# Split weights woven in pairs of chunks, and 64 bytes of padding behind the token-major tile

## The reference, cut to what matters

```
q, k, v, ga, uf, gf, zc, bc, cc, gc = split_cols(hx @ w_in, PROJ_SIZES)   # 1024 x 2816
a, b = jnp.split(h @ w_in, 2, axis=-1)                                    # 1024 x 5632
return (jax.nn.silu(a) * b) @ w_out                                       # 2816 x 1024
yx, yc = even_mixer(...)    # in: 1024 x 3088, out: 1024 x 1024
yx, yc = odd_mixer(...)     # in: 1024 x 3104, out: 1024 x 1024
```

## Time and profile before

| | |
|---|---|
| median of three runs | 2315.22 us |
| the profiled execution's own time, first to last instruction (its span) | 2314.2 us |
| TensorE matmuls busy | 2227.1 us, 19320 instructions |
| weight loads busy | 2091.2 us, 19320 instructions |
| VectorE busy | 1145.4 us |
| ScalarE busy | 846.8 us |
| GpSimd busy | 176.3 us |
| mean granted TensorE clock | 0.987 |
| share of the DMA queue that loads the weights | 46.1% of 16 engines' span |

### The profile page before, as it was taken

The page is one execution under the profiler, slowest core; times in us unless marked ns, Lnnn a source line. Parts: engine busy times, 40 slices in busy tenths (PEclk is TensorE's granted clock), DMA queues, the critical chain, the costliest instruction groups (busy, mean ns, idle before and its releaser), DMA issues. The chain is left out here.

```text
span 2314.2 us, 46991 instructions
## 1 busy us (share of the span) xinstructions
PE 2227.1 (96%) x19320; PEld 2091.2 (90%) x19320; DVE 1145.4 (49%) x1930; ACT 846.8 (37%) x1384; POOL 176.3 (8%) x150
## 2 busy tenths in 40 slices
PE   6999999899999999998999999999999999999998
PEld 5986798799999999976999999999999998979998
DVE  5227375653433445456653333454343446487665
ACT  4226454632221233248432222243232234455444
POOL 0003112100000010501200000010000010001000
PEclk9999999999999999999999999999999999999999
DMA  9853544445676244520354666242233233225573
GB/s 297 234 167 86 172 133 104 128 147 154 186 216 186 86 131 117 149 80 28 102 175 141 190 207 189 84 126 85 81 114 94 86 96 101 74 82 146 168 202 112
DMA packets 515900, 315.76 MB, mean 136 GB/s; under 512 B 16035, under 2 KB 513274, under 8 KB 515622
## 3 DMA queue, kind: packets, MB, share of 16 engines
q1 hardware_dynamic: 515160, 313.45, 46.1%
q10 hardware_dynamic: 590, 0.16, 0.0%
HBM read 312.50 MB, written 1.06 MB: 135 GB/s over the span
## 5 line engine op out<-in xcount | busy, mean ns | idle before, releaser
L1118 PE MATMUL ps<-h_hi,w_hi 128*128 128x256 f32 x3376 | 728.0, 280 | 3.5 <-DVE h_lo L1726 1.7
L1118 PE MATMUL ps<-h_lo,w_hi 128*128 128x256 f32 x3376 | 720.6, 278 | 0.0
L1118 PE MATMUL ps<-h_hi,w_lo 128*128 128x256 f32 x3376 | 720.6, 278 | 0.0
L1118 PEld LDWEIGHTS ps<-h_hi,w_hi 128*128 128x128 f32 x3376 | 537.8, 189 | 22.9 <-issue 21.6
L1118 PEld LDWEIGHTS ps<-h_lo,w_hi 128*128 128x128 f32 x3376 | 539.4, 189 | 0.1
L1118 PEld LDWEIGHTS ps<-h_hi,w_lo 128*128 128x128 f32 x3376 | 537.9, 189 | 0.0
L1960 DVE TENSOR_TENSOR w_lo<-stage,w_hi 128x1024 fp32r<-128x1024 f32 x227 | 285.0, 1258 | 441.5 <-ACT w_hi L1467 440.9
L1467 ACT ACTIVATE w_hi<-stage 128x1024 fp32r<-128x1024 f32 x227 | 236.6, 1055 | 334.4 <-PE ps L1118 200.4
L1960 DVE TENSOR_TENSOR w_lo<-deep,w_hi 128x1024 fp32r<-128x1024 f32 x184 | 226.1, 1234 | 226.9 <-ACT w_hi L1467 225.2
L1467 ACT ACTIVATE w_hi<-deep 128x1024 fp32r<-128x1024 f32 x184 | 191.9, 1055 | 179.7 <-PE ps L1118 141.4
L1118 PE MATMUL ps<-g_hi,w_hi 128*128 128x256 f32 x1100 | 232.9, 280 | 0.2
(11 more groups left out here) (413 smaller groups left out, 2858.0 us busy)
## 6 DMA issues: line engine op xcount, KB each, us to landing
modw<-in_ada_w SPq DMA_DIRECT2D x72, 1024.0 KB, 6.7
stage<-in_ffn_w_in SPq DMA_DIRECT2D x88, 512.0 KB, 3.9
deep<-in_ffn_w_in SPq DMA_DIRECT2D x88, 512.0 KB, 3.9
modw<-in_w_mod SPq DMA_DIRECT2D x18, 1024.0 KB, 6.1
stage<-in_w_in SPq DMA_DIRECT2D x30, 512.0 KB, 5.3
stage<-in_ffn_w_out SPq DMA_DIRECT2D x32, 384.0 KB, 3.5
stage<-in_even_w_in SPq DMA_DIRECT2D x24, 512.0 KB, 4.0
deep<-in_ffn_w_out SPq DMA_DIRECT2D x32, 384.0 KB, 3.4
```

The source lines that it names most:

```text
L1118: last = mm(ps[:, j, v - a:v - a + SEQ], w_part[wp][:, u % RING, c, :], x_part[xp][:, x, v:v + SEQ], start=first and wp == xp and v == a, ...
```

## The change

`sizes["vtok"]` grows by 16 words (64 bytes). Everything placed behind vtok moves up by 64 bytes and then begins on a multiple of 128 bytes, like the tiles ahead of it.

In the slots of `w_hi` and `w_lo`, chunks 2d and 2d+1 of a unit share 256 words: word 2n of them is column n of chunk 2d, word 2n+1 column n of chunk 2d+1. ScalarE and VectorE write them so, with a step of 8 bytes, and VectorE reads `w_hi` so; the landed weights in `stage` are read in sequence as before. Each stationary read of 128 columns then steps by 8 bytes and goes over 1024 bytes. The units of the token-major products keep the old layout. Neither the number of instructions nor a wait is changed.

```
-        sizes = {..., "vtok": TT * D + TT * ML_HEADS, ...
+        sizes = {..., "vtok": TT * D + 2 * TT * ML_HEADS, ...
+        token_units = {u for q in phases if q.kind == "gemm" and q.kw["evac"] == "tok"
+                       for u in range(q.at("unit_done"), q.at("unit_done") + 2 * q.kw["n"])}
+        def woven(x):
+            return x.rearrange("p c n -> p (c n)").rearrange("p (d n s) -> p d s n", s=2, n=P)
+        def split_out(u, x):
+            return x if u in token_units else woven(x)
+        def split_in(u, x):
+            return x if u in token_units else x.rearrange("p (d s) n -> p d s n", s=2)
+        def stationary(part, slot, c):
+            return woven(part[:, slot])[:, c // 2, c % 2, :]
...
# at L863, L962, L993, L1035, L1065 and L1118, with each one's slot and chunk:
-  last = mm(ps[...], w_part[wp][:, u % RING, c, :], x_part[xp][:, x, v:v + SEQ], ...
+  last = mm(ps[...], stationary(w_part[wp], u % RING, c), x_part[xp][:, x, v:v + SEQ], ...
...
-            up(act(w_hi[:, u % RING], slot, ACT.Copy), "w_hi", rounds)
+            up(act(split_out(u, w_hi[:, u % RING]), split_in(u, slot), ACT.Copy), "w_hi", rounds)
...
-            up(V.tensor_tensor(w_lo[:, u % RING], arrival(u)[0], w_hi[:, u % RING].bitcast(F32), ALU.subtract), "w_ready", rounds)
+            up(V.tensor_tensor(split_out(u, w_lo[:, u % RING]), split_in(u, arrival(u)[0]), split_out(u, w_hi[:, u % RING].bitcast(F32)), ALU.subtract), "w_ready", rounds)
```

More of the change, by code:

```diff
@@ L357, in sb @@
             return stack.enter_context(nc.sbuf_tensor(name, shape, dt))
-        sizes = {"resid": KC * NT, "big": 24 * NT, "hT": KC * NT, "mixT": KC * NT, "vtok": TT * D + TT * ML_HEADS, "stage": STAGE * KC * P,
+        sizes = {"resid": KC * NT, "big": 24 * NT, "hT": KC * NT, "mixT": KC * NT, "vtok": TT * D + 2 * TT * ML_HEADS, "stage": STAGE * KC * P,
                  "scr": 2 * RING * KC * P, "modw": 2 * KC * SEG,
@@ L862, in part @@
                         for v in range(0, NT, SEQ):
-                            last = mm(ps[:, u, v:v + SEQ], w_part[wp][:, u % RING, c, :], x_part[xp][:, c, v:v + SEQ],
+                            last = mm(ps[:, u, v:v + SEQ], stationary(w_part[wp], u % RING, c), x_part[xp][:, c, v:v + SEQ],
                                       start=c + v == 0 and wp == xp, stop=c == KC - 1 and wp == "lo", skip_group_check=True)
@@ L961, in pe_cross @@
                         for wp, xp in W_X:
-                            last = mm(ps[:, k, cols], w_part[wp][:, (u0 + k) % RING, c, :], x_part[xp][:, c, cols],
+                            last = mm(ps[:, k, cols], stationary(w_part[wp], (u0 + k) % RING, c), x_part[xp][:, c, cols],
                                       start=n == 0 and wp == xp, stop=n == KC - 1 and wp == "lo")
@@ L992, in pe_head @@
                             for wp, xp in W_X:
-                                last = mm(ps[:, bank, j * SEQ:(j + 1) * SEQ], w_part[wp][:, (u0 + 2 * q + j) % RING, n, :], x_part[xp][:, n, cols],
+                                last = mm(ps[:, bank, j * SEQ:(j + 1) * SEQ], stationary(w_part[wp], (u0 + 2 * q + j) % RING, n), x_part[xp][:, n, cols],
                                           start=n + j == 0 and wp == xp, stop=n == KC - 1 and wp == "lo", skip_group_check=True)
@@ L1034, in pe_seam @@
                             for wp, xp in W_X:
-                                last = mm(ps[:, 2 + j, cols], w_part[wp][:, u % RING, n, :], t_part[xp][:, x, cols],
+                                last = mm(ps[:, 2 + j, cols], stationary(w_part[wp], u % RING, n), t_part[xp][:, x, cols],
                                           start=x == 0 and wp == xp, stop=x == sum(ks) - 1 and wp == "lo")
@@ L1064, in pe_seam @@
                         for wp, xp in W_X:
-                            last = mm(ps[:, bank, part], w_part[wp][:, u % RING, n, :], x_part[xp][:, n, cols],
+                            last = mm(ps[:, bank, part], stationary(w_part[wp], u % RING, n), x_part[xp][:, n, cols],
                                       start=n == 0 and wp == xp and (k["dst"] is not None or j == 0), stop=n == KC - 1 and wp == "lo", skip_group_check=True)
@@ L1117, in chunk @@
                     for v in range(a, b, SEQ):
-                        last = mm(ps[:, j, v - a:v - a + SEQ], w_part[wp][:, u % RING, c, :], x_part[xp][:, x, v:v + SEQ],
+                        last = mm(ps[:, j, v - a:v - a + SEQ], stationary(w_part[wp], u % RING, c), x_part[xp][:, x, v:v + SEQ],
                                   start=first and wp == xp and v == a, stop=final and wp == "lo", skip_group_check=True)
```

## The result

The changed kernel takes 2404.05 us (median of four, 2403.55 to 2405.99) against 2315.2 us (median of four, 2311.31 to 2327.14). The ratio is 1.0371, 95% interval 1.0344 to 1.0398. The profiled execution of the changed kernel has a span of 2401.8 us, 87.6 above that of before.

The account below looks back on a forecast made before the run. The prediction took TensorE's spacing of matmul starts as the bound: 2315 us less 23 (all matmuls at 113.3 ns) and 3 (token-major products), other terms 0, gives 2289 us; range 2250 to 2345, own range 2280 to 2300.

Parts of the forecast that it names:

- What bounds the kernel: Whole kernel: the time is TensorE's, set by the spacing of matmul starts, mean 114.9 ns; waits are worth little.
- The floors: Weight-stationary matmuls: a 128-column load alone needs 111.4 ns, the moving stream 113.3; 117.8 adds a collision with the load.
- Address of the weights: Stationary reads moved 64 bytes to the moving reads' residue of 128: close spacing expected; token-major products alone -3 us.
- Weave: Stationary loads over 1024 instead of 512 bytes: nearly the moving stream's pace, so hardly any collisions; -23 us with the residue.
- Two streams at one pace keep their distance: Load beside moving stream: at equal pace they collide hardly at all or steadily; the first was expected.
- Reading with a step: Stationary reads stepping 8 bytes: taken as 0, 1.9 ns to spare; bound above, a load twice as long, +1,440 us.
- Writing with a step: ScalarE's and VectorE's stepped split writes: taken as 0; if doubled, VectorE would set the end's pace, +24 us.
- The landing address: DMA weight loads landing 64 bytes further on: taken as 0; a tenth either way in the first slices, 12 us.
- S: Every weight load with its matmul: the woven load costs TensorE time, 2358 us, or 2424 at 122.1 ns; chance 0.22.
- F: Weight-stationary matmuls: 113.3 ns is also a collision that equal pace removes, leaving the load's 111.4; -53 us, 2262; chance 0.18.
- N: Weight-stationary matmuls: only a reshuffle of close and wide spacing, set by restarts, not addresses; 2315 us, 2305 to 2325; chance 0.22.

Follow-up runs that it names:

- pad_only: The kernel before with only the 64 bytes of padding behind vtok, weights dense; 2375.9 us, ratio 1.0244.
- weave_only: The kernel before with only the two-chunk weave of the stationary weights, tiles where they were; 2392.7 us, ratio 1.0318.
- bcast_dense: The kernel before, with each main-loop matmul's moving operand one activation column repeated 256 times (step 0); 2279 us.
- pad_192: The kernel before with 192 bytes of padding behind vtok, weights dense, distance 0 modulo 256; dense windows at 120.2 and 119.9 ns a matmul.
- bcast_pad: The kernel before with the 64 bytes of padding, dense weights, and one moving column repeated 256 times in the main loop; 2281 us.
- short_woven: The changed kernel, padding included, with main-loop matmuls multiplying only the first 128 of each 256 tokens; 2607 us.

## Why the prediction was wrong, step by step

*What bounds the kernel* was right: nothing but TensorE's spacing moved, and 15,120 x the change of the mean step gives the change of the span within 4 us here. pad_only confirms it (15,120 x 3.9 = 59 us, span 58 longer), and so does weave_only (77 and 76).

*The floors.* The load's 111.4 ns was right; bcast_dense has 111.6. "I take 113.3 as the moving stream's own rate" stays open. With the loads as before but nothing travelling the spacing falls to the load's, which takes the travel away and doesn't say what it costs by itself; no run shows a travelling stream of 256 columns held below 113.3, and `wgate` has 113.2 with half the loads. (Counted again, 5,110 steps of the kernel before are of 115 to 120 ns and not 5,177; the mean stays 114.9.)

*Address of the weights* failed in its sign. The prediction put the good place at equal residues of 128 bytes, on 24 matmuls with `wgate` against 24 with `wlr`. The period is 256, the padding makes a distance of 128, and that costs 3.9 ns a matmul. Even the true reading of `wgate`, distance 0 modulo 256, would have misled, as pad_192 showed. Those 24 matmuls move 512 columns, the kernel's 15,120 move 256. For its own form the pair of rows even had the sign right: the mean of `wlr`'s 23 steps went from 232.4 to 229.5 ns with the padding alone (230.9 in weave_only, with the old addresses). Carrying it over to the other form is what failed. By itself this edit is +59 us (pad_only), in the place of the -23 that it shared with the weave. The token-major products, for which only the addresses change, went from 117.8 to 118.7 ns a step, so their -3 us didn't come either.

*Weave.* "Two streams at one pace keep their distance" led to a gain; no run shows one. At distance 64 the weave costs 5.1 ns a matmul, and without a travelling stream 6.2. That it adds only 2.1 ns when the padding is there too says that the two losses overlap in part; how isn't shown.

*Reading with a step*: taken as 0, with 1.9 ns to spare. This is the other step that failed: it costs the load 6.2 ns, a term of 15,120 x 5.1 = +77 us with the old addresses. The bound above, a load twice as long, belongs to a step of 16 bytes.

*Writing with a step* was right in its effect: ScalarE +0.10 us, VectorE 0, and TensorE's idle time (span less busy) is 85 us, where it was 87. The landing address shows nothing: bcast_pad and bcast_dense, which differ by the padding, are 2281 and 2279 us.

*The rivals.* S had 0.22 and named the place, each load with its matmul. Its mechanism is half right: the load is longer by itself, and the padding adds a loss that needs both streams; 121 ns lies between its 117.8 and 122.1. F's premise, that 113.3 is a collision too, stays open; either way the change doesn't bring 111. N is excluded: the changed kernel has no step of 112 to 114 ns.

## What to carry to other kernels

Where each matmul brings its own weight load and the load fills its time, as here, keep the stationary read dense: a step of 8 bytes took the load's spacing from 111.6 to 117.8 ns, one of 16 bytes the kernel's to 235.8. The distance between the stationary and the moving tile, modulo 256 bytes, is a tuning parameter worth up to 3% here; changing the size of any tile between them can move it unseen, so after an innocent edit look at the spacing of starts before looking for waits. A rule of addresses drawn from one form of matmul shouldn't be carried over to another.

## What was not expected of the hardware

Less work was slower. With 128 moving columns instead of 256 in the main loop, short_dense took 2524 us. The clock in its slices, and a window at its end:

```profile
PEclk9999955999999999999999999999999797555555
```

```profile
2310.00:2490.00 180.00, 180.00 (x846) 0.50 0.34 100
```

In two early slices and in the last six the clock is granted at half (1.2 GHz); in the window weight loads and matmuls follow each other without a gap, and the spacing is 180.00/844 = 213 ns instead of 111.6. Between them the engine ran the same kind of stream at full clock for 24 slices of 63 us. At full clock the eight slow slices would have taken some 240 us less (an estimate, 8 x 63 us x (1 - 111.6/213)); that gives about 2284 us, near the 2279 of bcast_dense. short_woven has the same half clock near its end, so only their windows at full clock are compared above. What the throttle answers to wasn't tried.
